# Processing 64 experts in pairs (t, t+16), (t+32, t+48) instead of (e, e+1)

## The reference

```python
def route(h, w_router, e_bias):
    T = h.shape[0]
    scores = jax.nn.sigmoid((h @ w_router).astype(jnp.float32))
    biased = scores + e_bias.astype(jnp.float32)
    grp = jnp.sum(lax.top_k(biased.reshape(T, N_GROUP, N_EXPERTS // N_GROUP), 2)[0], -1)
    _, gidx = lax.top_k(grp, TOPK_GROUP)
    gmask = jnp.any(gidx[:, :, None] == jnp.arange(N_GROUP)[None, None, :], axis=1)
    emask = jnp.repeat(gmask, N_EXPERTS // N_GROUP, axis=1)
    _, idx = lax.top_k(jnp.where(emask, biased, -jnp.inf), TOP_K)
    ...
    def expert_group(args):
        tok, wt, e = args
        xb = h_pad[tok]
        hid = jax.nn.silu(xb @ w1[e]) * (xb @ w3[e])
        return (hid @ w2[e]) * wt[:, None]
```

```
experts  0 to  7:  0 3 3 1 1 0 3 0
experts  8 to 15:  1 1 1 0 0 0 1 1
experts 16 to 23:  1 0 1 1 0 2 0 2
experts 24 to 31:  0 1 1 2 0 0 0 0
experts 32 to 39:  0 0 0 0 1 0 0 1
experts 40 to 47:  0 1 1 1 0 0 0 0
experts 48 to 55:  0 0 0 0 1 0 0 0
experts 56 to 63:  0 1 1 1 0 0 1 1
```

## Time and profile before

| what | value |
|---|---|
| median of 3 runs | 1399.9 us (1399.59 to 1402.65) |
| the profiled execution's own time | 1397.0 us |
| its span | 1395.2 us |
| TensorE (PE) busy | 1042.0 us, 75% |
| VectorE (DVE) busy | 445.8 us, 32% |
| ScalarE (ACT) busy | 232.1 us, 17% |
| GpSimd (POOL) busy | 219.2 us, 16% |
| HBM read | 331.25 MB |
| mean granted TensorE clock | 0.912 of full speed |

### The profile page before, as it was taken

One profiled execution on the slowest core, in us unless ns is written; L12 is line 12 of the kernel. 1 busy time (PEld: TensorE's weight loads), 2 busy tenths in 40 slices (PEclk: granted clock), 3 DMA queues, 4 the chain that ended last, 5 costly groups with the idle time before them and its releaser, 6 DMA issues. The chain is left out here.

```text
span 1395.2 us, 23612 instructions
## 1 busy us (share of the span) xinstructions
PE 1042.0 (75%) x8373; PEld 668.1 (48%) x8374; DVE 445.8 (32%) x829; ACT 232.1 (17%) x468; POOL 219.2 (16%) x369
## 2 busy tenths in 40 slices
PE   3289999996677599768688877878874784558862
PEld 2287887875566244344354444444442442234421
DVE  4323233335943112876122111111110111011148
ACT  1122222233555100011111111111100110001100
POOL 0001121100000000000233322223221222122213
PEclk9999999997699799958899999989997998789987
DMA  8575867541035593067357789998799999999473
GB/s 292 132 235 192 295 232 251 176 158 68 1 137 183 185 268 112 30 265 264 105 189 281 260 316 385 381 352 322 288 348 399 391 398 391 403 380 382 166 275 138
DMA packets 98507, 349.67 MB, mean 251 GB/s; under 512 B 15125, under 2 KB 20437, under 8 KB 73742
## 3 DMA queue, kind: packets, MB, share of 16 engines
q1 hardware_dynamic: 82862, 315.56, 62.1%
q0 software_dynamic: 13856, 30.13, 6.7%
q10 hardware_dynamic: 1728, 3.15, 0.6%
HBM read 331.25 MB, written 29.59 MB: 259 GB/s over the span
## 5 line engine op out<-in xcount | busy, mean ns | idle before, releaser
L1606 PE MATMUL PS<-W,XT 128*32 128x256 f32 x2048 | 135.8, 424 | 79.4 <-DMA W<-w 62.4
L1606 PEld LDWEIGHTS PS<-W,XT 128*32 128x32 f32 x2048 | 82.5, 122 | 146.6 <-issue 124.1
L1621 PE MATMUL PS<-W,XTo 128*64 128x256 f32 x1216 | 140.1, 383 | 0.0
L1621 PEld LDWEIGHTS PS<-W,XTo 128*64 128x64 f32 x1216 | 93.7, 138 | 43.3 <-issue 10.5
L428 DVE TENSOR_TENSOR w_lo<-raw,w_hi 128x2048 fp32r<-128x2048 f32 x26 | 59.5, 2289 | 147.3 <-ACT w_hi L390 147.3
L361 PE MATMUL PS<-w_hi,u_hi 128*128 128x512 f32 x240 | 95.9, 399 | 0.0
L361 PE MATMUL PS<-w_hi,u_lo 128*128 128x512 f32 x240 | 94.7, 395 | 0.0
L361 PE MATMUL PS<-w_lo,u_hi 128*128 128x512 f32 x240 | 94.7, 394 | 0.0
L1637 PE MATMUL PS<-W,hidTo 128*64 128x512 f32 x304 | 81.4, 657 | 16.4 <-DVE hidTo L1720 12.9
L1712 DVE TENSOR_TENSOR hid<-sg,PS 64x256 f32<-64x256 f32 x32 | 19.7, 614 | 218.0 <-ACT sg L1683 218.0
L1662 PE MATMUL PS<-W,hidT 128*32 128x512 f32 x512 | 64.7, 623 | 26.9 <-issue 23.4
(11 more groups left out here) (323 smaller groups left out, 1534.5 us busy)
## 6 DMA issues: line engine op xcount, KB each, us to landing
W<-w SPq DMA_DIRECT2D x192, 1024.0 KB, 14.3
raw<-w_in SPq DMA_DIRECT2D x26, 1024.0 KB, 9.4
oaT<-w_ada SPq DMA_DIRECT2D x8, 1536.0 KB, 7.8
G<-expert_rows SPq DMA_DIRECT2D x24, 512.0 KB, 12.8
obT<-w_ada SPq DMA_DIRECT2D x8, 512.0 KB, 8.1
kc<-cache_k_diff SPq DMA_DIRECT2D x8, 512.0 KB, 4.7
vc<-cache_v_diff SPq DMA_DIRECT2D x8, 512.0 KB, 3.7
Wa<-p_a SPq DMA_DIRECT2D x4, 1024.0 KB, 11.8
```

Source lines behind the costliest of these rows:

```text
L1606: mm = pe.matmul(PS[64 * h + 32 * c:64 * h + 32 * c + 32, UP_B + i, 0:F], XT[:, i, k, 32 * c:32 * c + 32], t.W13[:, 2 * i + c, h, k], star ...
L1621: mm = pe.matmul(PS[64 * h:64 * h + 64, XH_B, 0:F], XTo[:, k], t.W13[:, slot, h, k], start=k == 0, stop=k == KD - 1)
```

## The change

The pair n, with n = 2·it + i, is made of the experts it + 32i and it + 32i + 16, in place of 2n and 2n+1. So the pairs are (0, 16), (32, 48), (1, 17), (33, 49), ..., (15, 31), (47, 63). In routing a table `at_place` holds which expert stands at each place of this order; the one-hot table, the mask, the ranks, the counts, the numbers of the extra blocks and `ov` then go by place. The scores stay in the order of experts, and the product with them reads them in the order of places. The loads take the experts by `expert_at`.

```diff
+def expert_at(turn, slot):
+
+    return turn + E // WB * slot
...
+        at_place, at_place_i = sb("at_place", [P, E]), sb("at_place_i", [P, E], I32)
...
             for i in range(WB):
-                load_up(sp, t, i, i)
-                load_down(sp, t, i, i)
+                load_up(sp, t, expert_at(0, i), i)
+                load_down(sp, t, expert_at(0, i), i)
...
             pool.iota(io_i[:, :], pattern=[[1, P]], base=0, channel_multiplier=0).then_inc(iota_done, 1)
+            pool.iota(at_place_i[:, :], pattern=[[1, E // WB], [E // WB, WB]], base=0, channel_multiplier=0).then_inc(iota_done, 1)
...
-            dve.wait_ge(iota_done, 4)
+            dve.wait_ge(iota_done, 5)
             link(dve.tensor_copy(io[:, :], io_i[:, :]))
+            link(dve.tensor_copy(at_place[:, :], at_place_i[:, :]))
...
-                link(dve.tensor_tensor(oh[:, n], io[:, 0:E].unsqueeze(1).to_broadcast([P, TOPK, E]),
+                link(dve.tensor_tensor(oh[:, n], at_place[:, :].unsqueeze(1).to_broadcast([P, TOPK, E]),
                                        i8f[:, :].unsqueeze(2).to_broadcast([P, TOPK, E]), ALU.is_equal))
...
-                link(dve.tensor_tensor(tmp[:, :, :], oh[:, n], sc[:, n].unsqueeze(1).to_broadcast([P, TOPK, E]), ALU.mult))
+                sc_placed = sc[:, n].rearrange("p (s q) -> p q s", s=WB).unsqueeze(1).to_broadcast([P, TOPK, E // WB, WB])
+                link(dve.tensor_tensor(tmp[:, :, :].rearrange("p k (q s) -> p k q s", s=WB),
+                                       oh[:, n].rearrange("p k (q s) -> p k q s", s=WB), sc_placed, ALU.mult))
...
-                        load_up(sp, t, n * 2 + (c + WB), 2 * i + c)
+                        load_up(sp, t, expert_at(it + 1, 2 * i + c), 2 * i + c)
                     sp.wait_ge(yy_mm, n + 1)
                     stand_alone(sp)
                     for c in range(2):
-                        load_down(sp, t, n * 2 + (c + WB), 2 * i + c)
+                        load_down(sp, t, expert_at(it + 1, 2 * i + c), 2 * i + c)
```

## The result

| | before | after |
|---|---|---|
| median (lowest to highest, 4 runs each) | 1401.0 us (1399.59 to 1402.65) | 1384.4 us (1377.59 to 1389.16) |
| the profiled execution: time, span | 1397.0, 1395.2 us | 1389.2, 1387.4 us |
| stage of the experts in it, start to end | 682.7 to 1328.6, 645.9 us | 686.7 to 1321.0, 634.3 us |

The ratio is 0.990, interval 0.985 to 0.995: 16.6 us faster, where 26 were forecast. The profiled execution of the changed kernel is the slowest of its four runs and begins the stage 4.0 us late; about 3 of these are there before routing, in code that nobody touched. So the profile puts 7.8 us between the two executions.

The account below looks back on a forecast made before the run. TensorE and the weight-load queue were taken to limit the expert stage in turns; 28 us less waiting, 8 less slow restarts and 10.5 more work gave -26 on the median 1399.9, so 1374 us, range 1361 to 1388.

Parts of the forecast that it names:

- my ledger within some 6 us: Expert stage: pair-by-pair sum of start times from TensorE prices and weight landings, giving -26 us; chance 0.55.
- the first rival: Turning of later blocks' rows: late gathers eat the gain, likely half, -17 us, 1383; chance of half or more 0.22.
- last sign, pair 24 after 1200: Expert stage: the forecast is wrong if pair 24 starts after 1200 us in the timeline.
- waits for weights: TensorE's idle time before up-projections: 52 us in the ledger of before, 24 after, so 28 less.
- slow up-projections after them: Up-projection is 2 us longer after a wait of over 2 us; four such restarts fewer, 8 us less.
- more work: later blocks, heavy pairs under load: TensorE in the expert stage: 2.7 us for ten two-block pairs instead of eight, 3 times 2.6 for heavy pairs; 10.5 more.
- pair 2 starts at 707.4: Ledger of the changed order from 682.7: pair 2 starts then without waiting, its weights landed at 705.5.
- The queue's price: Weight-load queue: 6 MB a pair whatever its blocks, 17.4 us, midway between 16.8 and 17.9.
- The rival of spread addresses: Weight loads 16 MB apart run slower: no gain from 19.0 us a pair, +19 and 1419 at 20; chance 0.05.
- Pair 18 near 1025: Pairs 0 to 17 end near 1025 where pair 18 starts; later than 1040 means heavy pairs cost more.
- The rule of the Trainium skill: Row gathers under loads some 1.8 us longer, all 17 later blocks paying; 18 us, leaving 8 of the 26.
- Full cover: Expert stage: TensorE keeps unloaded prices and the queue is steady at 17.4, so -34 us, 1366; chance 0.17.

Follow-up runs that it names:

- the half loads: Only half of each weight tile loaded after the first four experts, matrix work unchanged, against the kernel before: changed order 1307.3 us, old order 1307.0, both ratio 0.935.
- swapped: The changed kernel with the two experts of each pair exchanged, (t+16, t), (t+48, t+32), so the heavy expert stands second: 1377.3 us, ratio 0.987 to the kernel before.
- the first experiment: The kernel before with only its weight loads in the changed sequence, routing, counts and blocks as before: 1398.6 us, ratio 1.001.
- The far pairs with early gathers: The changed kernel with pairs (t+32, t), (t+48, t+16) and two buffers for gathered rows of extra blocks: 1364.8 and 1362.2 us, ratios 0.979 and 0.977 to before.
- The kernel with the blocks alone: The changed kernel with its weight loads in the old sequence, against the kernel before: 1383.0 us, ratio 0.989.

## Why the prediction was right, and where it was off

The sign, the mechanism and the range held; the gain was 16.6 us and not 26. By the prediction's own cases that is outside of "my ledger within some 6 us" and at the size of the first rival, 17, though not by its reason. By the prediction's last sign, pair 24 after 1200, it would even be wrong: 1200.30, with 4.0 of it the late start of the stage. The best ledger of the stage is the one that the half loads allow. Whole stages by window: before, after, changed order with half loads, old order with half loads (columns as in rows 1).

```profile
682.70:1328.70 646.00, 481.63 (x4772) 269.42 (x4772) 108.71 (x210) 66.79 (x139) 160.90 (x273) 0.93 0.88 330
```
```profile
686.70:1321.00 634.30, 487.32 (x4772) 269.83 (x4772) 108.64 (x209) 66.78 (x139) 160.73 (x273) 0.93 0.90 336
```
```profile
680.20:1240.00 559.80, 456.47 (x4772) 261.66 (x4772) 108.62 (x209) 66.79 (x139) 160.72 (x273) 0.99 0.65 212
```
```profile
682.50:1242.10 559.60, 455.27 (x4772) 262.63 (x4772) 108.64 (x209) 66.89 (x139) 160.90 (x273) 0.99 0.64 212
```

The work itself takes 560 us in either order. The load traffic adds 86.4 before and 74.5 after. The same 4772 matmuls are busy 481.6 and 487.3 us, against 456: the rest is slow clock, 0.93 against 0.99. From before to after the stage changed by +5.7 busy and -17.4 idle. This table splits both and sets them against the terms of the prediction:

| term | forecast | profiled executions |
|---|---|---|
| waits for weights | -28 | -35.0, and +4.5 of ordinary gaps that had been hidden beneath them: -30.5 |
| slow up-projections after them | -8 | -3.0 (L1606 135.8, L1616 132.8 us busy) |
| more work: later blocks, heavy pairs under load | +10.5 | +8.1 waits for rows, +9.5 down-projections, by slow clock (81.4 to 87.2 and 64.7 to 68.4), +3.5 the stop ahead of pair 4, +0.7 the rest: +21.8 |
| stage | -26 | -11.7 |

The gaps are in these two groups, what ended TensorE's idle time before the up-projections, before (L1606) and after (L1616): us, times, longest.

```profile
PE PS L1606 <- issue: 17.0, 18, 1.5
```
```profile
PE PS L1616 <- issue: 25.0, 24, 4.3
```

They grew by 8.0. Of this 3.5 is the 4.30 ahead of pair 4 over the ordinary 0.8 behind a light pair; the other 4.5 are ordinary gaps. A pair that doesn't wait for weights still has its 0.8 to 1.3 us between down- and up-projection, so a wait that goes is worth that much less. The ledger had this in the pair's price, so that its -28 stands beside -30.5. It is also why its 52 us of waits for before were not short of the trace's 64.9, as the prediction has it: 14 waits each hold some 0.9 of gap.

The first line is right within 2.5; the other two together were forecast at +2.5 and came to +18.8. Not all of that is a miss of prices, as the ledger shows when it is laid beside the trace pair by pair:

| pairs | ledger of after | trace of after | |
|---|---|---|---|
| 0 to 4 | 109.8 | 123.4 | +13.6 |
| 5 to 16 | 221.9 | 220.8 | -1.1 |
| 17 and the wait of 18 | 10.3 | 17.6 | +7.3 |
| 18 to 23 (two blocks each) | 154.8 | 151.8 | -3.0 |
| 24 to the end | 127.2 | 120.7 | -6.5 |
| stage | 624.0 | 634.3 | +10.3 |

The ledger of before was 3.9 us too long (649.8 for 645.9), which makes up the 14.

**The step that was off** is "pair 2 starts at 707.4" and "pair 4 at 752.0", the first five pairs at the prices of pairs that came later. They started at 716.0 and 764.9, 4.0 of it the late start of the stage. Of the 13.6 us, 1.2 and 4.7 are in the heavy pairs 2 and 4, and 1.7, 2.9 and 3.1 in the light ones, 0, 1 and 3, which I had at 8.9 (and 15.8) like any other. The rows of pair 1 and of the last block but one of pair 2 show both kinds of loss:

```profile
711.66 0.44 PE L1662 MATMUL PS<-ident,hid 64*128 64x64 f32 x2 [3.14 <-issue]
712.64 3.64 PE L1672 MATMUL PS<-W,hidT 128*32 128x512 f32 x16 [0.54 <-issue]
...
735.77 1.08 PE L1622 MATMUL PS<-ident,hT 64*128 64x64 f32 x8 [3.43 <-DMA hT<-h_rows,ixo]
736.65 0.42 PE L1639 MATMUL PS<-ident,hido 64*128 64x64 f32 x2
737.50 3.68 PE L1647 MATMUL PS<-W,hidTo 128*64 128x512 f32 x8 [0.43 <-issue]
```

In pair 1 and ahead of pair 4 it is a stop of 3 to 4 us beside a fetch of instructions, then slow work behind it. In pairs 2 and 4 it is late gathers with the slow clock behind them. I had bounded the heavy pairs under load from 35.7 to 43.1; pair 4 took 45.2. And "four slow restarts fewer, 8 less" was 3.0, since such stops gave pairs 2 and 4 slow up-projections of their own.

From pair 5 on the prices were right in sum: the six two-block pairs took 25.3 each where I had 25.8. Singly they were not. Pair 12, with three blocks, took 31.0 and not 35.7, with the DMA engines at 0.80 over its length, so 35.7 is not the price of every three-block pair beside loads. In the -1.1 of the pairs 5 to 16 its -4.7 is set off in part by the two-block pairs 9 and 10, 27.2 and 27.1. The waits for rows (+8.1) and the slow down-projections (+9.5) are real, and of their 17.6 the forecast had 10.5. The first rival, later blocks dearer than in the ledger, did not come true there; what came in its place was the start.

**Two readings.** The prediction set 3.15 us of wait "with the queue full" (818.24) against 0.74 "with the queue quiet" (745.78). The queue was not quiet there. Two loads had been issued at 737.8, and the gather itself at 739.57; the engines in the kernel before were at

```profile
740.00:745.00 5.00, 5.00 (x40) 3.10 (x36) 0.69 (x1) 0.00 (x0) 1.75 (x3) 1.00 0.93 380
```

So these two rows don't give the price of load traffic. The half loads do: of the 10 waits, 19.9 us, in the stage of the old order none is left. And at 20 us a pair on the queue the ledger's own steps give +14 (1414), not +19 (1419); the addresses cost nothing, so it bore on nothing.

**The queue's price.** 17.4 us a pair was drawn from stretches with few blocks. Between 960 and 1040, where the changed order has the pairs 13 to 17, gathers and scatters take 13.2% of the engines' time; between 1221 and 1306, with few blocks, 6.1%:

```profile
q1 hardware_dynamic: 3748, 27.29, 88.7%
q0 software_dynamic: 1520, 3.54, 13.2%
```
```profile
q1 hardware_dynamic: 4452, 32.45, 94.7%
q0 software_dynamic: 1033, 1.74, 6.1%
```

The first is 960 to 1040: 27.29 MB in 80 us, so the 6.29 MB of a pair take 18.4 us. The second is 32.45 MB in 85 us, 16.5. This is a part of why pair 18 waited 10 us where the ledger had 1.4: at 18.4 a pair the ledger gives 5.4. Most of the wait goes with the order of the slots, which the ledger does not know: swapped, 2.4 are left. It also fits that 26 to 28 waited 5.2 each and not 6.5. The two errors, +7.3 and -6.5 in the table above, nearly cancel, and that is luck. The rival of spread addresses is ruled out by the first experiment, at 1.001.

**What had been named as signs.** Waits for weights 20 to 35: 29.9. Waits for rows 30 to 40: 31.2, so the first rival's own sign, over 50, did not come. Pairs 26 to 28 17 apart: 17.2 and 15.0. Pair 18 near 1025: 1048.5, beyond the 1040 that was to say that heavy pairs cost more. But of these 23.8 us 4.0 are the late start of the stage, 7.7 lie in the light pairs 0, 1 and 3, 7.3 are the wait of pair 18, and only 5.9 are the heavy pairs 2 and 4. As a sign for dearer heavy pairs it was too coarse, and the bound for pair 24 was passed for the same reasons.

**The rule of the Trainium skill.** The HBM Reference, section Latency, gives 0.2 us for an access on the average and 2 us under high load, so by an estimate from it 1.8 us more. Halving the bytes took 1.4 us off a gather, 7.6 to 6.2 (2.1 in the old order, 7.7 to 5.6), so the direction and about the size agree. The prediction's reading that all 17 later blocks would pay it in the new order does not hold: there are 14 waits in place of 11, and 8.1 us more, where the estimate from it had 18. No kernel here ran without loads.

**Full cover**, the rival at 1366, needed TensorE to keep unloaded prices beside full loads, for a stage of some 612 us (646 - 34). The changed kernel's took 634.3. The far pairs with early gathers came to 613.5 and 613.4, still with 18 to 19 us of waits for rows.

Still open: the stage accounts for 11.6 of the 16.6 us. The kernel with the blocks alone has a stage of 635.9 us, so 10.0 less than before's. The rest lies outside the stage or in the scatter between executions (the interval of the ratio reaches from 8 to 21 us), and no profile here assigns it.

## What to carry to other kernels

Where two limits take turns, price the work of each at the load that the new order will put beside it: a gather that is covered while the queue rests can be late when loads run, and then costs its wait and often the slow clock behind it. To find out whether a difference between two orders is overlap or work, run both with half of the bytes: if they are then equal, it is overlap. And a removed wait is worth its length less the ordinary gap that lay beneath it.

## What the runs showed of the hardware

- Behind 10 of the 13 late gathers in the stage the next down-projection ran at a slow clock: after 2.39 us of idle time the granted clock fell to 0.50, the lower of its two levels, and two down-projections took 2.73 and 3.64 us. Behind a gather that was 1.35 us late (949.74) the down-projection took its usual 1.94.
- Loads 16 MB apart run as fast as adjacent ones (1.001, 0.998 to 1.003).
- Gathers and scatters by index share the loads' engines: with them at 13.2% the loads moved 27.29 MB in 80 us (341 GB/s), with them at 6.1% 32.45 MB in 85 us (382 GB/s).
- Instructions are fetched over the DMA engines (queues q8 and q14). Stops of TensorE of 4.30, 3.14 and 2.82 us fall beside such fetches, but not every fetch has one. With half loads the stop ahead of pair 4 was still 3.73, so the weights' traffic doesn't make that one; the one in pair 1 was gone.
- SyncE's queue goes by program order: with the heavy expert's slot first the reloads of a three-block pair began 23.5 us after its start, with it second 4.7, and the DMA engines were at 0.76 and 0.97.
